# Modulation matvec in column strips of the array, and most of its units moved into the projections and the attention maps

## What is computed

```
c_act = silu(c); cc_act = silu(c_ctx)
for l in range(2):
    mod = c_act @ ada_w[l] + ada_b[l]            # 1 x 6144: sh1, sc1, g1, sh2, sc2, g2
    h = x * (1 + sc1) + sh1                      # 256 tokens
    if l == 0:
        mod_c = cc_act @ ada_w[0] + ada_b[0]
        hc = x_ctx * (1 + csc1) + csh1           # 256 context tokens
        y = even_mixer(h, hc, attn_w_in, ...)    # projections, two kinds of attention
    else:
        y = conv_mixer(h, ...)
    x = layer_norm(ALPHA * x + g1 * y)
    x = layer_norm(ALPHA * x + g2 * mlp(x * (1 + sc2) + sh2))
```

## Time and profile before

| | |
|---|---|
| median of three runs | 2346.26 us |
| span of the profiled execution, first to last instruction | 2342.4 us |
| PE busy | 2105.7 us (90%) |
| DVE, ACT, POOL busy | 1007.9, 936.0, 969.6 us (41 to 43%) |
| mean granted TensorE clock | 0.945 of full speed |
| bytes read from HBM | 335.27 MB |

### The profile page before, as it was taken

One profiled execution on the slowest core, in us unless ns is written; L12 is line 12 of the kernel. 1 busy time (PEld: TensorE's weight loads), 2 busy tenths in 40 slices (PEclk: granted clock), 3 DMA queues, 4 the chain that ended last, 5 costly groups with the idle time before them and its releaser, 6 DMA issues.

```text
span 2342.4 us, 36400 instructions
## 1 busy us (share of the span) xinstructions
PE 2105.7 (90%) x12952; PEld 1752.3 (75%) x12952; DVE 1007.9 (43%) x1576; ACT 936.0 (40%) x1517; POOL 969.6 (41%) x546
## 2 busy tenths in 40 slices
PE   6999799879998979978997888999999767999998
PEld 1264232379998879978776768999999756888887
DVE  0002532343342543341363111999200477676766
ACT  0010121134444244434533214556565665444443
POOL 0000000014445324435733005888878787444443
PEclk8999899999999989999997888999999888999999
DMA  7731344335543425533421224555555201555554
GB/s 213 247 128 62 108 144 135 135 107 181 181 160 134 144 101 185 180 137 142 162 91 63 97 101 144 179 180 182 185 179 180 81 0 45 187 187 187 188 189 155
DMA packets 93822, 338.69 MB, mean 145 GB/s; under 512 B 10272, under 2 KB 12616, under 8 KB 93384
## 3 DMA queue, kind: packets, MB, share of 16 engines
q1 hardware_dynamic: 90432, 329.29, 40.3%
q10 hardware_dynamic: 3336, 8.64, 1.3%
HBM read 335.27 MB, written 2.62 MB: 144 GB/s over the span
## 4 chain that ended last, share of the span: by engine, by line
PE 80%; DVE 9%; issue 4%; POOL 3%; DMA 2%; ACT 1%; POOLq 0%; ACTq 0%; DVEq 0%; SPq 0%
PE ps L382 32%; PE ps L894 10%; PE ps L675 8%; PE ps L365 8%; PE ps L900 5%; PE ps L452 4%; DVE arena L1298 2%; POOL h L1846 2%; DMA ring<-stream 2%; PE ps L400 2%; PE ps L649 2%; PE ps L423 2%; PE ps L531 1%; PE ps L509 1%; PE ps L618 1%
## 5 line engine op out<-in xcount | busy, mean ns | idle before, releaser
L326 POOL TENSOR_TENSOR ring_lo<-ring,ring_hi 128x1024 fp32r<-128x1024 f32 x350 | 852.4, 2442 | 1340.3 <-ACT ring_hi L320 1339.5
L320 ACT ACTIVATE ring_hi<-ring 128x1024 fp32r<-128x1024 f32 x476 | 502.8, 1057 | 351.9 <-DMA ring<-stream 347.0
L382 PE MATMUL ps<-h_lo,ring_hi 128*128 128x256 f32 x2176 | 315.4, 289 | 7.2 <-DVE h_lo L1450 7.2
L382 PEld LDWEIGHTS ps<-h_lo,ring_hi 128*128 128x128 f32 x2176 | 289.6, 197 | 8.7 <-DVE h_lo L1450 8.7
L937 ACT ACTIVATE arena<-ps 128x256 f32 (+2 forms) x245 | 95.0, 388 | 414.1 <-PE ps L382 260.1
L894 PE MATMUL ps<-late_r,ring_hi 128*128 128x512 f32 x1024 | 256.5, 392 | 2.0 <-ACT late_r L1183 2.0
L1795 DVE TENSOR_TENSOR late_r<-arena,late_r 128x256 fp32r<-128x256 f32 x128 | 173.9, 1360 | 108.9 <-ACT late_r L1183 108.9
L894 PEld LDWEIGHTS ps<-late_r,ring_hi 128*128 128x128 f32 x1024 | 184.2, 189 | 35.2 <-issue 2.3
L365 PE MATMUL ps<-arena,ring 128*128 128x256 f32 (+1 forms) x720 | 181.9, 416 | 16.9 <-DVE arena L1556 5.5
L382 PE MATMUL ps<-arena_r,ring_hi 128*128 128x256 f32 x1024 | 158.9, 301 | 31.1 <-DVE arena_r L1446 29.6
L365 PEld LDWEIGHTS ps<-arena,ring 128*128 128x128 f32 x720 | 141.6, 198 | 55.8 <-issue 23.8
(11 more groups left out here) (209 smaller groups left out, 2365.4 us busy)
## 6 DMA issues: line engine op xcount, KB each, us to landing
ring<-stream SPq DMA_DIRECT2D x628, 512.0 KB, 3.2
bias_rows<-late ACTq DMA_DIRECT2D x1, 1536.0 KB
arena<-decay ACTq DMA_DIRECT2D x1, 1536.0 KB, 6.5
resid<-x_t ACTq DMA_DIRECT2D x1, 1024.0 KB
arena<-ctx_t ACTq DMA_DIRECT2D x1, 1024.0 KB
late<-bias_rows ACTq DMA_DIRECT2D x1, 1024.0 KB, 7.9
out<-resid ACTq DMA_DIRECT2D x2, 512.0 KB, 2.6
cst<-consts ACTq DMA_DIRECT2D x1, 968.0 KB
```

The source lines that it names most:

```text
L320: act.activation(ring_hi[:, s, :], ring[:, s, :], ACT.Copy).then_inc(hi_ready, 1)
L326: eng.tensor_tensor(ring_lo[:, s, :], ring[:, s, :], ring_hi[:, s, :], ALU.subtract).then_inc(lo_ready[s], 1)
L382: m = pe.matmul(ps[:, bank, 0:T], w[:, kc * P:(kc + 1) * P], x[:, kc, :], start=begin, stop=w is w_lo and kc == KC - 1)
```

## The change

The eight matmuls of a modulation group now write to four different strips of 32 output partitions: row slice kc goes to strip kc mod 4. For this `cact` is 128 x 32 for each slice, with zeros in 30 of the columns, and two matmuls accumulate in each strip. The copy to `mod_row` takes all 128 partitions, and the four small matmuls sum the strips as they turn the row into columns, with the constant `pair` (128 x 2, ones where the partition mod 32 is 0 or 1) in place of the identity.

Only 16 of the 96 units (`sh1` and `sc1` of layer 0) stay ahead of the projections. The other 80 are 20 blocks of four units: eight blocks lie between the projection's units (after units 1, 3, 5, 7, 9, 11, 13 and 15), twelve lie in the even steps of the attention. The groups before the attention and before the output projection are gone. The host packs the stream in the new order; its number of units, its bytes and SP's program are the same.

```diff
-EARLY_ADA = 40
-STAGES = [("ada0", EARLY_ADA), ("attn_in", 18), ("ada_late", 2 * ADA_UNITS - EARLY_ADA), ("attn_out", 8), ("mlp0", 64),
+EARLY_ADA = 16
+BLOCK = 4
+N_LATE = (2 * ADA_UNITS - EARLY_ADA) // BLOCK
+WITH_ATTN_IN = 8
+STAGES = [("ada0", EARLY_ADA), ("attn_in", 18 + BLOCK * WITH_ATTN_IN), ("ada_late", BLOCK * (N_LATE - WITH_ATTN_IN)),
...
+BLOCK_AFTER = (1, 3, 5, 7, 9, 11, 13, 15)
+ATTN_IN_ORDER = [_x for _t in range(18) for _x in [("tile", _t)] + [("ada", BLOCK_AFTER.index(_t) * BLOCK + _q)
+                 for _q in range(BLOCK) if _t in BLOCK_AFTER]]
+ATTN_IN_UNIT = {_x: FIRST_UNIT["attn_in"] + _k for _k, _x in enumerate(ATTN_IN_ORDER)}
+
+
+def ada_late_unit(n):
+    if n < BLOCK * WITH_ATTN_IN:
+        return ATTN_IN_UNIT["ada", n]
+    return FIRST_UNIT["ada_late"] + n - BLOCK * WITH_ATTN_IN
...
-        cact = sb("cact", [P, KC, 2])
+        cact = sb("cact", [P, KC, 32])
...
+            def ada_strips(bank, unit_of):
+
+                for k4 in range(BLOCK):
+                    w = unit_of(k4)
+                    for k2 in range(2):
+                        kc = 2 * k4 + k2
+                        strip = 32 * (kc % 4)
+                        m = pe.matmul(ps[strip:strip + 32, bank, :], cact[:, kc, :], w[:, k2 * 512:(k2 + 1) * 512],
+                                      start=kc < 4, stop=kc >= 4)
+                        if k2 == 0:
+                            m.then_inc(units_begun, 1)
+                m.then_inc(full[bank], 1)
+                fills[bank].add()
+
+            def ada_sums(bank, rows):
+
+                for q in range(4):
+                    m = pe.matmul(ps[:, bank, 2 * q:2 * q + 2], rows[:, q * P:(q + 1) * P], const("pair", 2),
+                                  start=True, stop=True)
+                m.then_inc(full[bank], 1)
+                fills[bank].add()
+
             def ada_rows(u, i=None, between=None):
 
                 for g in range(2):
                     start_fill(4 + g)
-                    for k4 in range(4):
-                        w = unit(u + 4 * g + k4, i)
-                        for k2 in range(2):
-                            kc = 2 * k4 + k2
-                            m = pe.matmul(ps[0:2, 4 + g, :], cact[:, kc, :], w[:, k2 * 512:(k2 + 1) * 512],
-                                          start=kc == 0, stop=kc == KC - 1)
-                            if k2 == 0:
-                                m.then_inc(units_begun, 1)
-                    m.then_inc(full[4 + g], 1)
-                    fills[4 + g].add()
+                    ada_strips(4 + g, lambda k4: unit(u + 4 * g + k4, i))
...
+                    ada_sums(6 + g, mod_row[:, g, :])
...
-            def ada_units(m):
-
-                if m % 2 == 0:
-                    start_fill(7)
-                for n in (2 * m, 2 * m + 1):
-                    w = unit(FIRST_UNIT["ada_late"] + n)
...
+            def ada_columns():
+
+                pe.wait_ge(emptied[7], fills[7].now())
+                ada_sums(7, mod_row[:, 0, :])
+
+            def ada_block(n):
+
+                if n > 0:
+                    ada_columns()
+                start_fill(7)
+                ada_strips(7, lambda k4: unit(ada_late_unit(BLOCK * n + k4)))
+
+            def ada_between(step):
+
+                if step % 2 == 0:
+                    ada_block(WITH_ATTN_IN + step // 2)
+
+            def projections():
+
+                tile_unit = lambda t: ATTN_IN_UNIT["tile", t]
+
+                def ada_after(t):
+                    if t in BLOCK_AFTER:
+                        ada_block(BLOCK_AFTER.index(t))
+
+                for t in range(8):
+                    k_tile(tile_unit(t), lambda kc: hcat[:, kc, T:2 * T], 4 + t % 2)
+                    ada_after(t)
+                for t in range(8, 12):
+                    k_tile(tile_unit(t), lambda kc: hcat[:, kc, :], 4 + t % 2)
+                    ada_after(t)
...
+                for k4 in range(4):
+                    w = unit(tile_unit(12 + k4))
...
+                    ada_after(12 + k4)
...
-            ada_units(0)
-            ada_units(1)
...
-                      lambda m: ada_between(m + 2, 28) if m < 8 else None)
+                      lambda m: ada_between(m) if m < 8 else None)
...
-                      lambda m: ada_between(m + 10, 26))
+                      lambda m: ada_between(m + 8) if m < 16 else None)
...
-            ada_units(26)
-            ada_units(27)
...
-                    act.activation(mod_row[0:2, g, :], ps[0:2, 4 + g, :], ACT.Copy).then_inc(emptied[4 + g], 1)
+                    act.activation(mod_row[:, g, :], ps[:, 4 + g, :], ACT.Copy).then_inc(emptied[4 + g], 1)
...
+            dve.memset(cact[:, :, :], 0.0).then_inc(cact_zero, 1)
...
-                dve.tensor_copy(mod_row[0:2, 0, :], ps[0:2, 7, :]).then_inc(emptied[7], 1)
+                dve.tensor_copy(mod_row[:, 0, :], ps[:, 7, :]).then_inc(emptied[7], 1)
...
+            for n in range(WITH_ATTN_IN):
+                if n > 0:
+                    late_columns(n - 1)
+                late_row()
...
-            late_row()
...
+    put("pair", np.arange(P)[:, None] % 32 == np.arange(2)[None])
...
-        wide(a["ada_w"][0])[:EARLY_ADA],
-        tiles(aq), tiles(bq), tiles(ak), wide(v), tiles(bk), tiles(bvw),
-        wide(a["ada_w"][0])[EARLY_ADA:], wide(a["ada_w"][1]),
+        ada[:EARLY_ADA], np.stack([attn_in[n] if kind == "tile" else late[n] for kind, n in ATTN_IN_ORDER]),
+        late[BLOCK * WITH_ATTN_IN:],
```

More of the change, by code:

```diff
@@ L266, in build @@
         bias_in = sem("bias_in")
+        cact_zero = sem("cact_zero")
         cact_ready = sem("cact_ready")
@@ L460, in ada_columns @@
             def ada_columns():
                 pe.wait_ge(emptied[7], fills[7].now())
[L463 to L471, removed]
-                    ada_columns()
-                if m < last:
-                    ada_units(m)
@@ new lines, in ada_block @@
+            def ada_block(n):
+                if n > 0:
+                    ada_columns()
+                start_fill(7)
[14 more added lines that the diff above has]
+                    ada_after(t)
+                for tt in range(4):
+                    start_fill(tt)
+                for k4 in range(4):
+                    w = unit(tile_unit(12 + k4))
+                    for k2 in range(2):
+                        kc = 2 * k4 + k2
+                        for tt in range(4):
+                            m = pe.matmul(ps[:, tt, :], hcat[:, kc, tt * P:(tt + 1) * P],
+                                          w[:, k2 * 512:(k2 + 1) * 512], start=kc == 0, stop=kc == KC - 1)
+                            if k2 == 0 and tt == 0:
+                                m.then_inc(units_begun, 1)
+                            elif kc == KC - 1:
+                                m.then_inc(full[tt], 1)
+                    ada_after(12 + k4)
+                for tt in range(4):
+                    fills[tt].add()
+                k_tile(tile_unit(16), lambda kc: hcat[:, kc, :], 4)
+                w = unit(tile_unit(17))
@@ L498, in projections @@
                 fills[6].add()
[L500 to L511, removed]
-                                m.then_inc(units_begun, 1)
-                            elif kc == KC - 1:
-                                m.then_inc(full[tt], 1)
-                for tt in range(n_tok):
-                    fills[tt].add()
             def h_v_units(u, h_hi):
@@ L565, in _ @@
             wait_h()
-            projections(None, None)
+            projections()
             pe.wait_ge(emptied[4], fills[4].now())
```

40 lines of the change are left out of this document (15 added, 25 removed).

## The result

The changed kernel takes 2428.9 us (median of 4 runs, 2424.06 to 2430.55) against 2344.77 us of the kernel before in the same runs: ratio 1.0356, 95% interval 1.0318 to 1.0394. The profiled execution has a span of 2426.5 us, 84.1 us over the 2342.4 us of before. The forecast was slower by 35 us, with a range that ended at 2408: the direction was right, the size less than half, and the time lies 21 us above the range. Of the rivals none came: the clock did not stay up, the strips did overlap, and nothing was faster.

What follows compares the result with a forecast made beforehand. PE, busy 90% of the span, was taken as the bound. Terms summed to -12 us at full clock, then +37, +8 and +2 for the clock: +35 us, forecast 2382 us (median), range 2322 to 2408 us.

Steps and rivals of the forecast that it cites:

- the clock did not stay up: Rival: clock stays at 0.9 or more in the attentions, 2334 to 2344 us, no change; chance 0.27.
- the late load in every block: Sign: in every block PE idles 2 to 3 us, ending with a load of the stream.
- 1 ahead of the projections: Before the projections: 24 units go, -49.3 us, and shorter matmuls save some 6 us; term -55 us.
- 2 projections, full clock: Projections: eight added blocks of 5.3 us plus a 0.6 us wait each, and seven sums of 1.05 us; +55 us.
- 3 head norms: Before the attention: the modulation group between DVE's last step and the scores goes; -7.6 us.
- 4 first attention, full clock: First attention: a pair of steps goes from 14.75 to 16.3 us, times four; +6 us.
- 5 second attention, full clock: Second attention: a pair of steps goes from 15.5 to 14.3 us, times eight; -10 us.
- 8 clock in the attentions: Both attentions: mean clock falls to 0.75, half the time at 1.2 GHz, 6.2 us a pair; +37 us.
- 8 clock in the projections: Projections: PE stays 77% busy, and the clock costs 1 us per block; +8 us, ends 0 and 16.
- 8 up to the MLP: Output projection: starts after 8 us with little on PE, where modulation had kept it warm; +2 us.
- The rival of no overlap: Rival: column strips run one after another, +23 us at full clock, up to +40, 2370 to 2387 us; chance 0.13.
- The rival *faster: Rival: ahead of the projections most of 15 us of load waits also goes; 2321 us; chance 0.10.

Runs made afterwards that it cites:

- e3_fill: Changed kernel plus three zero-weight matmuls in each late block, ahead of the wait for its fourth unit; 2381.49 us, ratio 1.0166 to the kernel before.
- e7_fill_both: e3_fill plus zero matmuls in the attention's odd steps where PE waits for DVE, three (first attention) or one (second); 2365.66 us, ratio 1.0104.
- e2_one_load: Changed kernel with each of the 20 late blocks loading one unit and using it for all eight matmuls; 2317.01 us, ratio 0.9889.
- e8_spread_warm: e1_spread plus zero matmuls in the first attention, two in each odd step and one in each even step; 2282.27 us, ratio 0.9756.
- e1_spread: Changed kernel with blocks halved: two units behind each of the first 16 projection units and in every attention step; 2286.29 us, ratio 0.9734.

## Why the prediction was right in direction and too small

Of the signs that the prediction named, the late load in every block came, and pairs of 21.0 us in the first attention and 19.9 in the second lie within its bounds. The projections took 175.8 us where it had put 155 to 165, and the clock in the attentions was under its 0.7 to 0.85. By its steps, in us against the profiled execution before:

| term | forecast | measured | from |
|---|---|---|---|
| 1 ahead of the projections | -55 | -51.0 | changed kernel |
| 2 projections, full clock | +55 | +63.5 | e3_fill, 162.0 - 98.5 |
| 3 head norms | -7.6 | -7.5 | changed kernel |
| 4 first attention, full clock | +6 | +11.1 | e7_fill_both |
| 5 second attention, full clock | -10 | -1.7 | e7_fill_both |
| 8 clock in the attentions | +37 | +48.8 | changed kernel less e7_fill_both |
| 8 clock in the projections | +8 | +13.8 | changed kernel less e3_fill |
| 8 up to the MLP | +2 | +7.9 | changed kernel |
| the rest of the kernel | 0 | -0.8 | changed kernel |
| sum | +35 | +84.1 | |

- The mechanism of term 2 was right: the fourth unit was asked for 1.22 us after the block's start (1.20 forecast), and PE idled 2.74 us for it in the block shown (2.6). Three sizes were short. In e3_fill, from which the +63.5 comes, a block lasts 5.5 to 6.3 us from its first strip to its last (5.3 forecast), 4.5 us more for the eight. The next tile's unit was asked for 0.87 us after the fourth (0.4) and in the block shown landed after 5.2 us, longer than the longest of the earlier trace rows; in e3_fill these waits are 0.20 to 2.27 us, 7.1 us in all against 4.8. And the wait for DVE's bias add, 0.26 us ahead of seven blocks, was not in the sum: 1.8 us.
- Strips do overlap. Eight matmuls took 1.92 us, 3.7 times less than the 7.05 us in one strip, close to the 1.8 and 7.0 us of the forecast. The rival of no overlap is out. The page sentence on which it rested, in the Trainium skill (TensorE: Matmul & The Clock Gate, The mechanism), has a weight load pass a running matmul only where the row group differs; the trace of e2_one_load disagrees, since there the loads for the second round of strips run at 100.42 to 100.55 us, under matmuls on the same rows that run from 100.40 to 101.03. The same section of the Trainium skill also lets a weight load go ahead of running matmuls where it targets the background weight buffer. The prediction says that no run shows such an overlap yet; but in the earlier trace rows the projections have PE busy for 98.45 of 98.5 us and PEld for 60.09, so weight loads already ran beside matmuls on all 128 rows. The 2.38 times for three column tiles in the Trainium skill (same page, Measured speedup vs the span model) is 0.79 per tile; this kernel got 3.7 times for four, 0.92 per strip.
- **The step that failed is term 8, the clock that I took for the attentions.** I set it at 0.75, above the 0.70 of the nearest row, with the reason that there the idle time came in one piece of 13 us and here it would be spread. Spread idle time did not keep the clock up: it was 0.68 and 0.62, below the nearest row, and even the range ended at 0.65. The price of a lower clock was about right: by its 6.2 us a pair the measured clocks give an estimate of 44 us against the clocks of e7_fill_both and 54 us against a full one, and 48.8 us was measured. With the projections and the stretch up to the MLP term 8 was +70.5 where the forecast had +47: 23.5 of the 49 us that were missing. The rest is in terms 5 (8.3), 2 (8.5), 4 (5.1) and 1 (4.0).
- What lowers the clock so far is shown in part. Filling the idle pieces brought it back (e3_fill, e7_fill_both, e8_spread_warm), and taking away the load waits alone did not (e2_one_load). The busy share that the profile gives was a poor guide: the second attention is busy 82% in e1_spread at a clock of 0.98 and 82% in e2_one_load at 0.67. Both hold the same matmuls (x353), 69 us of them in e1_spread and 100 us in e2_one_load, where the lower clock draws them out; so its 82% is in part the loss itself, and so are the changed kernel's 68 and 75% over the 56 to 64% of full-clock work that I had reckoned. What differs between the two is where the strips lie, half of them in each step or all in the even one, how many units are loaded, and PE's wait for DVE in an odd step, 0.63 us against 1.63 us (row above). In e1_spread's first attention that wait is up to 2.18 us, and the clock 0.69. Whether the length of the idle piece or the share of full-clock work decides stays open, since no run changed one without the other.

```profile
280.75 1.11 PE L567 MATMUL ps<-cst,arena 128*128 128x128 f32 x4 [2.18 <-DVE arena L1382]
```

```profile
342.98 0.66 PE L567 MATMUL ps<-cst,arena 128*128 128x128 f32 x4 [0.63 <-DVE arena L1403]
```

- Terms 4 and 5 at full clock were 5 and 8 us short. In a pair of e7_fill_both's first attention that ran at full clock the even step took 11.97 us (11.35 forecast) and the odd one 4.89 (4.95): what was off is the block, 5.92 for 5.3. In four pairs that is 2.2 us. The rest of both differences may be the stretches at 1.2 GHz that e7_fill_both still had (clock 0.92 and 0.94) and the matmuls that it added; no run separates it.
- The term "up to the MLP" (+7.9) is again clock: 0.50 in the 13 us in which PE waits for DVE's norm and 0.81 after it, where the kernel before had a modulation group on PE and 1.00 and 0.98.
- The rival *faster*, more gain ahead of the projections, did not occur: ACT issued the table transfer at 26.38 us (27.00 before), and the units asked for behind it still came late. PE's timeline there:

```profile
51.55 1.92 PE L438 MATMUL ps<-ring,cact 128*32 128x512 f32 x4 [16.51 <-DMA ring<-stream]
...
62.16 3.18 PE L438 MATMUL ps<-ring,cact 128*32 128x512 f32 x8 [4.84 <-DMA ring<-stream]
```

They landed when they had landed before: PE went on at 51.55 and 62.16 us, in the kernel before at 51.41 and 62.18. So the faster matmuls only made the waits longer, 16.51 and 4.84 us against 11.20 and 3.80.

## What to carry to other kernels

When a piece of work gets faster, look at when its inputs are asked for. Here units were asked for three ahead and used in a burst of four, and the 5 us of PE time that a block saved came back as idle time, 2.5 us a block for its load; the same units used two at a time were 143 us faster than the burst. Work that looks like filler between dependent steps holds TensorE's clock up (0.98 and 0.94 with it in both steps, 0.70 and 0.67 in e2_one_load with it in one): before you take it out or gather it in one place, price every matmul behind the new idle time at 1.2 GHz. And if a test kernel with useless matmuls in the gaps is faster, the gaps are what to remove.

## What was not expected of the hardware

- Zero-weight matmuls in idle time made a kernel 47 us faster (e3_fill), and with those in the odd steps 63 us (e7_fill_both): the clock rose from 0.62 to 0.94 in the second attention.
- Four column strips of float32 matmuls with 512 moving columns each, every one of two records, ran almost wholly at once: 1.92 us for eight, in two rounds.
- Beside the 1.5 MB table transfer a 512 KB load took many times its usual time, in the kernel before as well (waits of 11.20 and 3.80 us in the earlier trace rows). From the issues of line 1865 (the loads of the stream), first 530 us of the changed kernel:

```profile
DMA to landing us min/median/max: 3.0/4.3/19.5
```

The smallest is 3.0 us as before. The 19.5 us are those of a load issued at 34.49 us, 8 us behind the table transfer, which landed at 54.01; the one before it, issued at 33.62 and landed at 51.50, is what ended the wait of 16.51 us above.
